# The chunks of an mLSTM mixer dealt in among the output-gate projections, in a fused fp32 transformer block

## The reference, cut to what matters

```python
mod = jax.nn.silu(c) @ ada_w[l] + ada_b[l]                 # 6 x 1024 modulation values
sh_m, sc_m, g_m, sh_f, sc_f, g_f = jnp.split(mod[:, None, :], 6, axis=-1)
h = rms_norm(x, norm_mix_pre[l]) * (1.0 + sc_m) + sh_m
(mq, mk, mv, mo, mi, mf, nq, kc, vc, ksl, vsl, kwn, vwn, ng) = split_cols(h @ w_in[l], IN_WIDTHS)
y_m = mlstm_mixer(mq, mk, mv, mo, mi, mf, ...)
k_c = compress_kv(rope(as_kv(kc), positions), ...)         # silu(blk @ w1) @ w2, the same for v_c
y_n = nsa_attention(q, k_c, v_c, ...)
y = jnp.concatenate([y_m, y_n], axis=-1) @ w_out[l]
x = x + g_m * rms_norm(y, norm_mix_post[l])
...
x = x + g_f * rms_norm(hier_moe(h, ...), norm_ffn_post[l])

# mlstm_mixer, for 4 heads of 128
qk = silu(causal_conv(concat(q_pre, k_pre), conv_w))       # 4 taps
wts = exp(dlog - m_t) * (q @ k^T)                          # decay matrix times scores, per chunk
num = wts @ v + dec * (q @ C_prev)                         # C: state, carried from chunk to chunk
h = rms_norm(num / max(|den|, exp(-m_t)))
return sigmoid(o_pre) * h
```

## Time and profile before

| | us |
|---|---|
| median of 3 runs (1594.56 to 1597.02) | 1596.22 |
| the profiled execution | 1597.23 |
| its span in the trace | 1595.4 |
| PE busy, share of the span | 1356.9, 85% |
| DVE busy | 631.6, 40% |
| ACT busy | 385.7, 24% |
| POOL busy | 76.5, 5% |
| mo projection ends, in the trace | 422.41 |
| attention begins, in the trace | 504.95 |

### The profile page before, as it was taken

How to read it: one execution, slowest core, us unless ns; L and a number is a source line. 1 busy time by engine, 2 the same in 40 slices (tenths; PEclk the granted TensorE clock), 3 DMA queues, 4 the chain that set the end, 5 groups by cost and what they waited for, 6 DMA issues and landing times.

```text
span 1595.4 us, 17126 instructions
## 1 busy us (share of the span) xinstructions
PE 1356.9 (85%) x6271; PEld 689.7 (43%) x6271; DVE 631.6 (40%) x1400; ACT 385.7 (24%) x873; POOL 76.5 (5%) x109
## 2 busy tenths in 40 slices
PE   2899999999876888998899955999989898898750
PEld 2744444444564444544445533444434343343320
DVE  5726424422046676666423344222232222222307
ACT  2334211101065655554232320000000000000005
POOL 0000000000013000000000000000000000000013
PEclk8899999999987999999999965999999999999975
DMA  9611222112320870000362262999999999999957
GB/s 337 144 53 54 93 106 105 53 53 106 123 89 5 236 240 1 1 1 1 124 245 79 79 263 96 365 391 401 382 399 393 410 395 394 392 393 405 418 193 290
DMA packets 109979, 331.40 MB, mean 208 GB/s; under 512 B 26172, under 2 KB 50376, under 8 KB 101320
## 3 DMA queue, kind: packets, MB, share of 16 engines
q1 hardware_dynamic: 97400, 299.86, 50.2%
q0 software_dynamic: 5712, 19.42, 3.6%
q10 hardware_dynamic: 6784, 11.02, 1.9%
HBM read 287.78 MB, written 42.49 MB: 207 GB/s over the span
## 4 chain that ended last, share of the span: by engine, by line
PE 28%; SPq 17%; DVE 6%; DMA 4%; issue 2%; ACT 2%; DVEq 0%; POOL 0%; ACTq 0%
SPq L637 14%; PE ps L1411 6%; PE ps L1451 5%; PE ps L1501 4%; PE ps L1462 3%; DMA arena<-expert_w 2%; PE ps L1317 2%; PE ps L1334 2%; PE ps L1354 2%; SPq L635 2%; SPq L683 1%; ACT arena L998 1%; PE ps L1396 1%; PE ps L1441 1%; DMA d_y<-arena 1%
## 5 line engine op out<-in xcount | busy, mean ns | idle before, releaser
L1462 PE MATMUL ps<-arena 128*32 128x256 f32 (+1 forms) x1408 | 198.4, 501 | 34.1 <-DMA arena<-expert_w 31.8
L1172 PE MATMUL ps<-arena 128*128 128x512 f32 x512 | 221.0, 593 | 0.0
L1501 PE MATMUL ps<-arena 128*32 128x256 f32 (+2 forms) x832 | 152.7, 498 | 4.3 <-issue 1.9
L1172 PEld LDWEIGHTS ps<-arena 128*128 128x128 f32 x512 | 96.9, 190 | 119.7 <-issue 119.6
L1179 PE MATMUL ps<-arena 128*128 128x512 f32 (+1 forms) x384 | 142.0, 530 | 1.2 <-ACT arena L843 1.2
L1462 PEld LDWEIGHTS ps<-arena 128*32 128x32 f32 (+1 forms) x1408 | 74.9, 127 | 143.6 <-issue 126.6
L1451 PE MATMUL ps<-arena 128*128 128x512 f32 x256 | 116.7, 614 | 7.9 <-DVE arena L2006 7.9
L1411 PE MATMUL ps<-arena 128*128 128x512 f32 x256 | 112.7, 592 | 0.1
L998 ACT ACTIVATE arena<-arena 128x640 f32<-128x640 f32 (+7 forms) x128 | 92.8, 727 | 59.2 <-DVE arena L1808 59.2
L1179 PEld LDWEIGHTS ps<-arena 128*128 128x128 f32 x384 | 72.3, 189 | 68.9 <-issue 62.1
L1334 PE MATMUL ps<-arena 128*128 128x128 f32 x528 | 79.9, 285 | 21.2 <-ACT arena L998 9.2
(11 more groups left out here) (318 smaller groups left out, 1315.4 us busy)
## 6 DMA issues: line engine op xcount, KB each, us to landing
arena<-expert_w SPq DMA_DIRECT2D x99, 2048.0 KB, 35.4
arena<-ada_w SPq DMA_DIRECT2D x12, 2048.0 KB, 9.2
d_y<-arena SPq DMA_DIRECT2D x24, 512.0 KB, 6.3
arena<-x SPq DMA_DIRECT2D x16, 512.0 KB, 4.4
arena<-w_in SPq DMA_DIRECT2D x4, 2048.0 KB, 12.9
d_y<-arena ACTq DMA_DIRECT2D x40, 128.0 KB
arena<-w_out SPq DMA_DIRECT2D x2, 2048.0 KB, 14.0
d_x<-arena SPq DMA_DIRECT2D x8, 512.0 KB, 2.6
```

The lines of the kernel that those rows point to most:

```text
L1172: last = nc.tensor.matmul(b, w(k), hT[:, k, 512 * c:512 * c + 512], start=(k == 0), stop=(k == KT - 1))
L1462: last = nc.tensor.matmul(ps[width * j:width * j + width, 2 if width == 64 else 3, 0:span], xgT[s][:, k, lo:lo + width], w_up[slots[n]][:, ...
L1501: last = nc.tensor.matmul(dst, hid_T[s][:, at_:at_ + width], w_down[slot][:, k, span * j:span * j + span], start=(k == 0), stop=(k == 3))
```

## The change

The barrier B is taken out. On PE the order becomes: mq and mk, now with the modulations 7 to 11 behind single tile pairs; the compression; mv; and then the chunks, each led by one mo tile. ACT does the exponentials of two chunks behind each of the mv tiles 4 to 7, and the Sigmoid of a gate tile at the head of each chunk. DVE does the modulation sums 7 to 11 behind the convolutions 0 to 4.

So that `hT` stays alive, the decay matrices move into ring slot 2 and the chunk's temporaries into ring slot 0 and the space of the rotation tables. Each ring item now names its slot: slot 2 takes ada 2, ada 4 to 11 one after the other and both compression weights; slot 0 mq and mv; slot 1 mk and mo; w_out takes slots 0 and 1 behind the chunks.

```diff
-    jobs += [("mq", j, c) for j in range(4) for c in range(CH)] + [("ada", 7)]
-    jobs += [("mk", j, c) for j in range(4) for c in range(CH)]
-    jobs += [("mv", t) for t in range(4)] + [("ada", 8)] + [("mv", t) for t in range(4, NT)] + [("ada", 9)]
-    jobs += [("mo", t) for t in range(NT)] + [("ada", 10), ("ada", 11)]
+    for j in range(4):
+        jobs += [("mq", j, c) for c in range(CH)] + [("ada", 6 + j)] * (j > 0)
+    for j in range(4):
+        jobs += [("mk", j, c) for c in range(CH)] + [("ada", 10 + j)] * (j < 2)
     jobs += [("chid", 0), ("chid", 1), "kcmp", "vcmp"]
+    jobs += [("mv", t) for t in range(NT)]
     jobs += [("S", 0), ("kr", 0)]
     for c in range(NT):
+        jobs += [("mo", c)]
         jobs += [("S", c + 1)] * (c + 1 < NT) + [("kr", c + 1)] * (c + 2 < NT) + [("num", c, p) for p in range(2)]
...
-    items = [ada_item(i) for i in range(4)]
+    items = [(i % 3, ada_item(i)) for i in range(4)]
...
+    items.append((1, [piece(0, OFF["kc"], 3 * P)]))
+    items += [(2, ada_item(5)), (2, ada_item(6)), (0, [piece(0, OFF["mq"], 512)]), (2, ada_item(7))]
+    items += [(1, [piece(0, OFF["mk"], 512)])] + [(2, ada_item(i)) for i in (8, 9, 10)]
+    items += [(0, [piece(0, OFF["mv"], 512)]), (2, ada_item(11))]
+    items.append((2, [(2048 * a, 0, d["cmp_w1_" + n].rearrange("(k p) n -> p k n", p=P)) for a, n in enumerate("kv")]))
+    items.append((1, [piece(0, OFF["mo"], 512)]))
+    items += [(i, [(0, 0, w_out[:, :, 512 * i:512 * i + 512])]) for i in range(2)]
...
-        bc = view(HT, MH, NT, P)
-        at = [4096]
+        bc = view(RING2, MH, NT, P)
+        at = [RING0]
...
-            sp.wait_ge(stage_end["B"], 4)
+            sp.wait_ge(psum_ready, JOB[("chid", 1)] + 1)
+            sp.wait_ge(hop_in, 96)
             sp.dma_start(bc, d_nmx.rearrange("r l -> (r l)").rearrange("(a n) -> a n", a=1).broadcast_to([P, 32 * P])
                          .rearrange("p (h c l) -> p h c l", h=MH, c=NT)).then_inc(decay_in, 16)
             sp.dma_start(a_old, d_old.rearrange("r a -> a r").broadcast_to([P, 32])).then_inc(decay_in, 16)
+            sp.wait_ge(stage_end["C"], 4)
...
-            end_stage(pool, "B")
-            nc.gpsimd.memset(state[0], 0.0).then_inc(state_zero, 1)
+            pool.wait_ge(psum_ready, JOB[("mv", NT - 1)] + 1)
+            nc.gpsimd.memset(state[0], 0.0).then_inc(state_zero, 1)
+            pool.wait_ge(conv_done, 8)
...
-            silu_conv(7)
-            act.wait_ge(roped, 14)
-            for t in range(NT):
-                b = ready(act, ("mv", t))
-                read(nc.scalar.activation(v1[:, t, :, 0:P], b.rearrange("p (h n) -> p h n", h=MH), ACT.Copy,
-                                          scale=MH_SCALE), ("mv", t))
-            act.wait_ge(hop_in, 96)
-            for t in range(NT):
-                b = ready(act, ("mo", t))
-                read(nc.scalar.activation(ym[:, t, :], b, ACT.Sigmoid), ("mo", t))
-            end_stage(act, "B")
+            silu_conv(7, mk_silu)
             for a in range(2):
                 act.wait_ge(hbias_ready, a + 1)
                 b = ready(act, ("chid", a))
-                read(nc.scalar.activation(hid[:, a, :, :], b[:, 0:P].rearrange("p (g n) -> p g n", g=2), ACT.Silu,
+                read(nc.scalar.activation(hid[a], b[:, 0:P].rearrange("p (g n) -> p g n", g=2), ACT.Silu,
                                           bias=hbias[:, a:a + 1]), ("chid", a))
             b = ready(act, "vcmp")
             for g in range(2):
                 rows = slice(HD * g, HD * g + NCMP)
                 last = nc.scalar.copy(v_pair[rows, g, :], b[rows, 0:HD])
             read(last, "vcmp")
-            for c in range(NT):
-                act.wait_ge(decay_masked, c + 1)
-                for h in range(MH):
-                    last = nc.scalar.activation(bc[:, h, c, :], bc[:, h, c, :], ACT.Exp,
-                                                bias=gcols[:, 0, 8 * h + c:8 * h + c + 1])
-                last.then_inc(decay_exp, 1)
+            act.wait_ge(roped, 14)
+            for t in range(NT):
+                b = ready(act, ("mv", t))
+                read(nc.scalar.activation(v1[:, t, :, 0:P], b.rearrange("p (h n) -> p h n", h=MH), ACT.Copy,
+                                          scale=MH_SCALE), ("mv", t))
+                for c in (2 * t - 8, 2 * t - 7) if t >= 4 else ():
+                    act.wait_ge(decay_masked, c + 1)
+                    for h in range(MH):
+                        last = nc.scalar.activation(bc[:, h, c, :], bc[:, h, c, :], ACT.Exp,
+                                                    bias=gcols[:, 0, 8 * h + c:8 * h + c + 1])
+                    last.then_inc(decay_exp, 1)
+            act.wait_ge(hop_in, 96)
+            def open_gate(c):
+                b = ready(act, ("mo", c))
+                read(nc.scalar.activation(ym[:, c, :], b, ACT.Sigmoid), ("mo", c))
             def weigh_keys(c):
...
+                open_gate(c)
...
-                if n == "mq":
-                    last_of(modulation(claim(pe, ("ada", 7)), 7, 0))
-            w = item(IT_MV)
-            for t in range(NT):
-                tokens(("mv", t), w, 0, 512, t)
-                if t % 4 == 3:
-                    last_of(modulation(claim(pe, ("ada", 8 + t // 4)), 8 + t // 4, 0))
-            w = item(IT_MO)
-            for t in range(NT):
-                tokens(("mo", t), w, 0, 512, t)
-            for i in (10, 11):
-                last_of(modulation(claim(pe, ("ada", i)), i, 0))
-            end_stage(pe, "B")
+                    a = 4 * i + j + 6
+                    if 7 <= a <= 11:
+                        last_of(modulation(claim(pe, ("ada", a)), a, 0))
             pe.wait_ge(const_in, 144)
+            item(IT_CMP)
...
+            w = item(IT_MV)
+            for t in range(NT):
+                tokens(("mv", t), w, 0, 512, t)
...
+            pe.wait_ge(mk_silu, 1)
             scores_and_keys(0)
+            pe.wait_ge(v1_ones, 1)
+            for t in range(NT):
+                was_read(pe, ("mv", t))
+            w_gate = item(IT_MO)
             for c in range(NT):
+                tokens(("mo", c), w_gate, 0, 512, c)
...
+                if i >= 8:
+                    dve.wait_ge(psum_ready, JOB[("ada", i - 4)] + 1)
...
-                    if m == 2:
-                        sum_modulation(7)
-                    if m == 3:
-                        modulation(7)
-            for i in (8, 10):
-                sum_modulation(i)
-                sum_modulation(i + 1)
-                modulation(i)
-                modulation(i + 1)
-            end_stage(dve, "B")
+                    if m <= 4:
+                        sum_modulation(m + 7)
+                    if 1 <= m <= 5:
+                        modulation(m + 6)
+            for i in range(10, 12):
+                was_read(dve, ("ada", i))
...
+                was_read(dve, ("mo", c))```

PE around the chunks, before: the gate tiles stand in one row (64 matmuls, the last of L1179), ahead of the compression (L1235) and chunks 0 to 2 (L1255 scores, L1260 key turn, L1267 num, kv and int).

```order
L1179 MATMUL ps<-arena 128x512 x64
L1138 MATMUL ps<-arena 128x1 x8
L1235 MATMUL ps<-arena 128x129 x32
L1241 MATMUL ps<-arena 64x63 x2
L1247 MATMUL ps<-arena 63x64 x2
L1255 MATMUL ps<-arena 128x128 x4
L1260 MATMUL ps<-arena 128x128 x4
L1255 MATMUL ps<-arena 128x128 x4
L1260 MATMUL ps<-arena 128x128 x4
L1267 MATMUL ps<-arena 128x129 x12
L1255 MATMUL ps<-arena 128x128 x4
L1260 MATMUL ps<-arena 128x128 x4
```

More of the change, by code:

```diff
@@ L228, in temp @@
             at[0] += int(np.prod(shape))
-            assert at[0] <= MKT
+            assert at[0] <= RING0 + 4096
             return v
         wts, kw = [temp(MH, P) for _ in range(2)], [temp(MH, P) for _ in range(2)]
-        num, inter = [temp(MH, P + 1) for _ in range(2)], [temp(MH, P + 1) for _ in range(2)]
+        num = [view(COS + 516 * i, MH, P + 1) for i in range(2)]
+        inter = [view(COS + 1032, MH, P + 1), temp(MH, P + 1)]
         state = [temp(MH, P + 1) for _ in range(2)]
-        junk_h = temp(MH, P)
+        junk_h = view(KCT + 256, MH, P)
         ident = tiny(P)
@@ L273, in build @@
         vec = view(V1 + 2048, P, parts=124)
-        hid = temp(2, 2, 64)
+        hid = [view(KCT + 1040 * a, 2, 64) for a in range(2)]
         pos_i, pos_f, ang, turns = view(MKT, S).bitcast(I32), view(MKT + S, S), view(MKT + 2 * S, S), view(MKT + 3 * S, S)
@@ L535, in was_read @@
             eng.wait_ge(bank_read[JOB[name] % 8], JOB[name] // 8 + 1)
[L537 to L540, removed]
+        ring_total, ring_want, ring_slot, ring_before = [0, 0, 0], [], [], []
+        for i, (slot_, pieces) in enumerate(ITEMS):
+            ring_before.append(max([n for n in range(i) if ring_slot[n] == slot_], default=None))
+            ring_slot.append(slot_)
+            ring_total[slot_] += 16 * len(pieces)
+            ring_want.append(ring_total[slot_])
         def end_stage(eng, k):
@@ L573, in load_ring @@
```

(21 more changed lines are left out.)

53 lines of the change are left out of this document (23 added, 30 removed).

## The result

The changed kernel takes 1569.22 us (median of 4 runs, 1567.29 to 1571.85) against 1596.62 (4 runs, 1594.56 to 1598.46). The ratio is 0.9834, 95% interval 0.9816 to 0.9851. So it is 1.7% faster, and the interval is clear of 1. Measured a second time on another chip, the same kernel took 1570.15 against 1596.41, ratio 0.9840 (0.9822 to 0.9858). The forecast was 1570.

A forecast was written before the change was run, and what follows sets the result against it. TensorE's waits and gaps between 422.41 and 504.95 us were taken as the bound. Terms -5.1 - 1.5 - 18.8 - 1.3 = -26.7 took 1597.2 to 1570.5; forecast 1570, own range 1565 to 1577, 8 in 10 for 1563 to 1580.

The forecast's parts named there:

- the moved point: Start of attention's first scores on TensorE, forecast at about 478 us, against 504.95 before the change.
- Wait for the compression weights and barrier: TensorE's 5.07 us wait for cmp_w_k ahead of the compression goes, as the load is issued earlier: -5.1 us.
- Compression: Its 64 entries run behind dense work at full clock, 0.216 us each: 13.8 us for 15.3, -1.5.
- Chunks: With a gate tile in each, TensorE sets the chunk at 11.09 us; own work 32.1 for 50.9: -18.8.
- The slack at the bank of the gate tile: In each chunk the Sigmoid frees the PSUM bank 1.8 us before TensorE's second int product needs it; cost 0.
- Decay matrices: The 32 ScalarE exponentials ahead of chunk 0 move behind value tiles 4 to 7, which cover them: cost 0.
- The side remark on the lost cover: Without the value tiles covering the exponentials, the 7.5 us of empty TensorE time come back.
- Tail: From the chunks' last products to attention: 7.2 us for 8.52, between 6.3 and 8.5; -1.3.
- Modulation chain: Ada 5 to 11 share slot 2; turns of 14.2 us against TensorE's 14.6; cost 0, bounds 0 and 15.
- Everything behind attention's start moves whole: Every microsecond by which attention starts earlier reaches the kernel's end; later stages are not tied to an absolute time.

The follow-up runs named there:

- six copies: The changed kernel with six more dependent ScalarE copies ahead of the Sigmoid in chunks 1 to 7; 1575.70 us, ratio 0.9883.

## Why the prediction was right

The time (1570 for 1569.22) and the moved point (478 for 478.22) came out, and so did the mechanism, but two terms were mis-sized in opposite directions: the compression came out 1.3 us dearer than forecast, the chunks 1.2 cheaper. That 26.7 met 26.73 to a tenth is luck.

- *Wait for the compression weights and barrier, -5.1:* as predicted. The load was issued at 282.79, and TensorE did not wait for it at 314.17.
- *Compression, -1.5:* mis-sized. It took 15.07 us (314.17 to 329.24) and not 13.8; before it was 15.26 (429.32 to 444.58), so -0.2. The failing step was 0.216 us an entry, read from 12 entries in a window of 2.6 us, where one entry more or less at the edges is 8%; all 64 in 15.3 us, partly at the lower clock, gave 0.24, and that was the figure to take: the rate did not depend on the clock, 10 entries in the 2 us from 431.3 at 0.50 and 10 in the 2 us from 437.3 at 1.00. The experiment with neighbouring elements shows that the stride sets it.
- *Chunks, 32.1 us of TensorE's work:* 30.9 (385.37 to 471.32 is 85.95, less eight tiles of 6.88), so -20.0 for -18.8. Scores and key turn are 1.33 and the 24 products 2.68 when nothing interrupts them; the rows of before that gave 1.44 and 2.76 were about 0.1 longer each, and no run shows why. That TensorE sets the chunk, at 10.89 for 11.09, held. The slack at the bank of the gate tile was 1.8 us in the prediction, with the Sigmoid's load starting when the tile is ready. It was 2.3: the load started 0.7 ahead of that, the Sigmoid ended at 438.37 (437.77 + 0.60), and TensorE came to the second int product at about 440.7 (an estimate: 438.46 and 20 of the 24 entries in 2.68 us). By the loops there were 2.6 us to spare.
- *Decay matrices, 0:* held. The side remark on the lost cover did not (2.3 us of waits for 7.5).
- *Tail, 7.2:* 6.9.
- *Modulation chain, 0:* held. The sum of ada 8 ended at 240.16 and its reading product was asked at 241.93, 1.8 us; the later ones had 2.3, 2.8 and 3.2, a lead that grew by 0.5 a turn. The load of ada 8 took 9.1 us (issued at 225.12, first used at 234.24), more than the 7.9 assumed, and its turn 15.1 us (sums ended at 225.02 and 240.16) for TensorE's 14.6; the next three turns took 14.1 to 14.2. So the margin was real, but thinner than the turn of 14.2 said.
- *Everything behind attention's start moves whole:* held within the scatter of the experts' stage (468.33 us for 468.70 to the first gather, 618.85 for 621.75 behind it).

ScalarE in one chunk of the changed kernel, the lines that answer to the earlier trace rows:

```profile
434.86 1.28 ACT L991 ACT_TABLE_LOAD   x1
436.16 0.30 ACT L991 ACTIVATE arena<-arena 128x4 f32<-128x4 f32 x1
436.47 1.28 ACT L956 ACT_TABLE_LOAD   x1
437.77 0.60 ACT L956 ACTIVATE arena<-ps 128x512 f32<-128x512 f32 x1
438.66 1.15 ACT L965 ACTIVATE arena<-ps,arena 128x128 f32<-128x128 f32 x4 [0.29 <-PE ps L1263]
```

There is no drain behind either load: Sqrt and Sigmoid follow 0.01 to 0.02 us behind its end, against the 1380 ns that the Trainium skill, "ScalarE: Activation LUTs", section "What ACT_TABLE_LOAD costs", adds. Nor is there one ahead: each load starts within 0.02 us of the end of the instruction before it. The rule of the Trainium skill, "ScalarE: Activation LUTs", to batch calls by set was broken here sixteen times at no cost to TensorE, whose work set the pace of the chunks. In the tail ScalarE is on the path, and there one load out of the way gave 1.06 us.

## What to carry to other kernels

Where a chain of small steps runs round several engines with TensorE waiting, deal independent dense tiles into it, one a turn, and count for each turn TensorE's work, the slowest other engine's loop, and the point at which a PSUM bank comes round. A second engine's extra work is free up to the difference of the two (2.6 us a turn here), and is passed on behind it: with six copies ScalarE, idle only for 1.18 us behind VectorE, set a turn of 12.02. Price a wait of TensorE of some 3 us at twice its length where nothing behind it waits anyway, and read rates from whole groups, not from windows of a few entries.

## What the runs showed of the hardware that was not expected

- fp32 matmuls with a moving operand of 129 columns at a stride of 8 elements took 0.235 us an entry at a granted clock of 1.00, and 0.24 in the stretch of before that began at 0.50 (mean 0.86); with neighbouring elements 0.113, at 1.00.
- The table load of the Sigmoid began at 436.47, before its gate tile was done (430.25, 16 entries, the next product at 437.14): the load did not wait for the activation's data, only the activation did. That is not general: ahead of attention's first exponential the load (L1009) began at 479.56, behind a wait of 3.06 us for VectorE.
- Behind waits of TensorE of 2.83 and 2.95 us the clock stood at 0.50 for about 6 us although the work was dense again. Behind the wait of 2.03 us in the run with the late exponentials it stayed at 1.00.
- Writing 256 fp32 columns in groups of eight that lie 130 elements apart, instead of side by side, cost VectorE 618 ns for 422 and ScalarE 620 for 367.
